# Wide weight tiles and four accumulator banks in the second part of each out projection, and a new slot order for the side work of the last mixer

## What is computed

```python
def second_block(x, norm_mix_w, w_in, ...):
    h = rms_norm_2(x, norm_mix_w)
    proj = h @ w_in                       # 45 column tiles of 128
    z, xbc, dt_raw, q, k, v, f_raw = split(proj)
    y_ssd = ssd_mixer(...)                # 16 heads; (y + d_skip*x) * silu(z), then a norm over two groups
    y_fox = fox_mixer(...)                # 16 heads; q, k normed per head, causal softmax with decays
    x = x + concatenate([y_ssd, y_fox]) @ w_out     # 16 input tiles of 128
    hf = rms_norm_2(x, norm_ffn_w)
    x = x + conv_gated_mlp(hf, w_up, conv_w, conv_b, w_down)

def first_block(x, mem, ...):             # layers 0 (retention) and 1 (differential attention)
    x = x + concatenate([o_main, o_mem]) @ w_out[layer]       # 8 input tiles
    h = rms_norm(x, ffn_norm_w[layer])
    x = x + (silu(h @ w_gate) * (h @ w_up)) @ w_down[layer]
```

## Time and profile before

| | |
|---|---|
| median of 3 runs | 1190.63 us (1189.59 to 1196.57) |
| profiled execution, its own time | 1190.49 us |
| its span (first to last instruction) | 1188.7 us |
| PE busy | 1091.9 us, 92% |
| DVE, ACT, POOL busy | 787.0, 610.2, 170.5 us |
| mean granted TensorE clock | 0.973 |

### The profile page before, as it was taken

The page is one execution under the profiler, slowest core; times in us unless marked ns, Lnnn a source line. Parts: engine busy times, 40 slices in busy tenths (PEclk is TensorE's granted clock), DMA queues, the critical chain, the costliest instruction groups (busy, mean ns, idle before and its releaser), DMA issues.

```text
span 1188.7 us, 23717 instructions
## 1 busy us (share of the span) xinstructions
PE 1091.9 (92%) x8466; PEld 1037.2 (87%) x8466; DVE 787.0 (66%) x1290; ACT 610.2 (51%) x1074; POOL 170.5 (14%) x186
## 2 busy tenths in 40 slices
PE   5999989999998987779999999988788898999999
PEld 5978879999998776679999999987677788999999
DVE  7664676666555785776665658867755648888853
ACT  7643554444544554364444546665544447666542
POOL 4000121111110001031111100000101003444400
PEclk9999989999999998889999999999988999999999
DMA  7522345555664222055555664442222236555563
GB/s 265 176 93 94 92 152 197 185 180 174 190 186 155 77 93 67 27 171 191 179 182 177 181 202 143 163 139 89 89 71 72 78 118 195 179 185 185 168 197 114
DMA packets 52775, 174.45 MB, mean 147 GB/s; under 512 B 5856, under 2 KB 9056, under 8 KB 52576
## 3 DMA queue, kind: packets, MB, share of 16 engines
q1 hardware_dynamic: 52704, 173.49, 45.3%
HBM read 172.42 MB, written 1.05 MB: 146 GB/s over the span
## 4 chain that ended last, share of the span: by engine, by line
PE 50%; DVE 12%; ACT 2%; issue 2%; POOL 0%; ACTq 0%; DVEq 0%
PE bank L561 15%; PE bank L562 15%; PE bank L563 15%; DVE ring_lo L1220 2%; PE bank L614 1%; DVE xw_lo L1226 1%; DVE bank L1367 1%; DVE bank L1365 1%; DVE u L1383 1%; DVE x L1275 1%; DVE negmax L1429 1%; PE bank L700 1%; ACT tmp L1054 1%; PE bank L627 1%; DVE tmp L1426 1%
## 5 line engine op out<-in xcount | busy, mean ns | idle before, releaser
L561 PE MATMUL bank<-xw_hi,ring_hi 128*128 128x256 f32 x1736 | 508.7, 293 | 8.2 <-DVE xw_lo L1226 3.4
L562 PE MATMUL bank<-xw_lo,ring_hi 128*128 128x256 f32 x1736 | 495.4, 285 | 0.0
L563 PE MATMUL bank<-xw_hi,ring_lo 128*128 128x256 f32 x1736 | 495.0, 285 | 0.0
L1220 DVE TENSOR_TENSOR ring_lo<-ring_raw,ring_hi 128x1024 fp32r<-128x1024 f32 (+3 forms) x353 | 399.9, 1136 | 50.1 <-ACT ring_hi L838 43.6
L838 ACT ACTIVATE ring_hi<-ring_raw 128x1024 fp32r<-128x1024 f32 (+3 forms) x353 | 345.0, 979 | 101.1 <-PE bank L563 97.0
L561 PEld LDWEIGHTS bank<-xw_hi,ring_hi 128*128 128x128 f32 x1736 | 337.9, 195 | 17.3 <-issue 10.1
L562 PEld LDWEIGHTS bank<-xw_lo,ring_hi 128*128 128x128 f32 x1736 | 337.7, 195 | 4.1 <-issue 3.9
L563 PEld LDWEIGHTS bank<-xw_hi,ring_lo 128*128 128x128 f32 x1736 | 337.1, 194 | 0.0
L561 PE MATMUL bank<-act_hi,ring_hi 128*128 128x256 f32 x848 | 250.1, 295 | 29.5 <-DVE ring_lo L1220 11.7
L562 PE MATMUL bank<-act_lo,ring_hi 128*128 128x256 f32 x848 | 245.2, 289 | 0.0
L563 PE MATMUL bank<-act_hi,ring_lo 128*128 128x256 f32 x848 | 244.9, 289 | 0.0
(11 more groups left out here) (159 smaller groups left out, 854.6 us busy)
## 6 DMA issues: line engine op xcount, KB each, us to landing
ring_raw<-w_up SPq DMA_DIRECT2D x132, 512.0 KB, 3.2
ring_raw<-w_in SPq DMA_DIRECT2D x85, 512.0 KB, 3.2
ring_raw<-w_down SPq DMA_DIRECT2D x48, 512.0 KB, 3.7
ring_raw<-w_down SPq DMA_DIRECT2D x24, 384.0 KB, 3.9
ring_raw<-w_oa SPq DMA_DIRECT2D x16, 384.0 KB, 3.1
ring_raw<-w_kv SPq DMA_DIRECT2D x8, 512.0 KB, 5.7
ring_raw<-w_oa SPq DMA_DIRECT2D x8, 512.0 KB, 3.5
ring_raw<-w_ob SPq DMA_DIRECT2D x16, 128.0 KB, 2.0
```

The lines of the kernel that those rows point to most:

```text
L561: mm(bank[b][:, 0:T], w_hi, tile(hi, t), start=kk == 0, stop=False)
L562: mm(bank[b][:, 0:T], w_hi, tile(lo, t), start=False, stop=False)
L563: last = mm(bank[b][:, 0:T], w_lo, tile(hi, t), start=False, stop=end)
L1220: V.tensor_tensor(ring_lo[:, a:b], ring_raw[:, a:b], ring_hi[:, a:b].bitcast(f32), SUB).then_inc(lo_done, 1)
```

## The change

It does four things.

1. `PHASES`: ob0 and ob1 have 2 ring tiles of 1024 columns instead of 8 of 256 (four outputs each), ob2 4 of 1024 instead of 8 of 512 (two outputs each). The bytes are the same.
2. ob has its own loops, `project_group` on PE and `group_into_stream` on ACT and DVE. DVE's order is now add of output m, then `xw_lo` of output m-1, with `split_lo` once for each ring tile, behind its last add. ACT's `split_hi` stands behind the square and copy of output `group // 2` of each ring tile.
3. kv, ob, up and down use banks 0 to 3 instead of 0 and 1 (`Phase.bank`), and PE waits for the output four back (`Phase.freed`). in and oa keep two banks.
4. `plans()`, layer 2: `ssd_skip` and `turn` keep their slots but stand first in them; `fox_probs` stands first in its slot or right behind a `norm_out`; `fox_weights`, `fox_values` and the attention's `mix` come one slot later; `group_norm` of the second group moves from slot 37 to 40, with `group_out` and its four `mix` steps (39 to 42).

```diff
-          ("in0", 20, [8], 20), ("oa0", 8, [6], 8), ("ob0", 8, [2], 4), ...
+          ("in0", 20, [8], 20), ("oa0", 8, [6], 8), ("ob0", 2, [8], 2), ...
-          ("in2", 45, [8], 45), ("oa2", 16, [8, 4], 16), ("ob2", 8, [4], 4), ...
+          ("in2", 45, [8], 45), ("oa2", 16, [8, 4], 16), ("ob2", 4, [8], 4), ...
+        self.group = 8 // n if name[:2] == "ob" else 1
+        self.banks = 2 if name[:2] in ("in", "oa") else 4
...
-        at(2, a + 3, "ssd_skip", p)
         at(2, a + 3, "ssd_gate", p)
...
-        at(2, a + 5, "turn", 36 + 2 * j)
-        at(2, a + 6, "turn", 37 + 2 * j)
         for n in range(2):
             p, slot = 2 * j + n, a + 7 + 3 * n
+            plan[2][a + 5 + n].insert(0, ("turn", 36 + p))
             at(2, slot, "fox_scores", p)
-            at(2, slot + 1, "fox_probs", p)
-            at(2, slot + 1, "fox_weights", p)
-            at(2, slot + 2, "fox_values", p)
-            at(2, slot + 3, "mix", 8 + p)
-    for g, slot in ((0, 28), (1, 37)):
+            plan[2][slot + 1].insert(0, ("fox_probs", p))
+            at(2, slot + 2, "fox_weights", p)
+            at(2, slot + 3, "fox_values", p)
+            at(2, slot + 4, "mix", 8 + p)
+    for p in range(8):
+        plan[2][20 + 2 * p].insert(0, ("ssd_skip", p))
+    for g, slot in ((0, 28), (1, 40)):
...
+            def project_group(layer):
+                ph = PH[f"ob{layer}"]
+                ks = DM // P // ph.group
+                for c in range(ph.n):
+                    slot, g = ph.tile(0, c)
+                    pe.wait_ge(lo_done, g + 1)
+                    for j in range(ph.group):
+                        m = ph.group * c + j
+                        n = ph.out0 + m
+                        b = bank[n % 4][:, 0:T]
+                        pe.wait_ge(out_ready, ph.freed_first(n, m))
+                        for k in range(ks):
...
+            def group_into_stream(layer, q):          # ACT
+                ph = PH[f"ob{layer}"]
+                for c in range(ph.n):
+                    for j in range(ph.group):
+                        m = ph.group * c + j
+                        act.wait_ge(out_ready, ph.out0 + m + 1)
+                        stream(q, m, x)
+                        if j == ph.group // 2:
+                            split_hi(ph, 0, c)
...
+            def group_into_stream(layer, q):          # DVE
...
+                        V.tensor_tensor(tile(x, m), tile(x, m), bank[(ph.out0 + m) % 4][:, 0:T], ADD).then_inc(out_ready, 1)
+                        if m:
+                            stream_lo(q, m - 1, x)
+                    split_lo(ph, 0, c)
+                stream_lo(q, KT - 1, x)
```

More of the change, by code:

```diff
@@ L123, in out, with bank, freed, freed_first @@
         return self.out0 + c // self.per + (self.body // self.per) * i
+    def bank(self, i, c):
+        n = self.out(i if type(i) is int else 0, c)
+        return n % self.banks
+    def freed(self, i, c):
+        n, j = self.out(i, c), c // self.per
+        if type(i) is int:
+            j += self.outs // self.turns * i
+        if self.banks == 2 or type(i) is not int and self.outs // self.turns < 4:
+            return n - 1
+        if type(i) is not int or j >= 4 or self.name[:2] in ("up", "do"):
+            return n - 3
+        return self.freed_first(n, j)
+    def freed_first(self, n, j):
+        if j >= 4:
+            return n - 3
+        b = n % 4
+        if b >= 2:
+            return n - j if self.name != "kv" else 0
+        before = self.out0 - 1
+        return (before if before % 2 == b else before - 1) + 1
 def phases():
@@ L545, in project @@
                 n = ph.out(i, c)
-                b = (ph.out0 + c // ph.per) % 2
+                b = ph.bank(i, c)
                 part = c % ph.per
@@ L549, in project @@
                 pe.wait_ge(lo_done, g + 1)
-                if part == 0 and not (first and n < 2):
-                    pe.wait_ge(out_ready, n - 1)
+                if part == 0:
+                    freed = ph.freed(i, c)
+                    if not (type(freed) is int and freed <= 0):
+                        pe.wait_ge(out_ready, freed)
                 last = None
@@ L564, in project @@
                 last.then_inc(tile_done, 1)
+            def project_group(layer):
[10 more added lines that the diff above has]
+                        for k in range(ks):
+                            t = ph.inputs[k]
+                            if m == 0:
+                                pe.wait_ge(mix_lo, number["mix", (layer, t)] + 1)
+                            a = slot * DM + (j * ks + k) * P
+                            w_hi, w_lo = ring_hi[:, a:a + P], ring_lo[:, a:a + P]
+                            mm(b, w_hi, tile(act_hi, t), start=k == 0, stop=False)
+                            mm(b, w_hi, tile(act_lo, t), start=False, stop=False)
+                            last = mm(b, w_lo, tile(act_hi, t), start=False, stop=k == ks - 1)
+                        if j < ph.group - 1:
+                            last.then_inc(ob_done, 1)
+                        else:
+                            last.then_inc(tile_done, 1)
             def mean_square(q):
@@ L1122, in _ @@
                 run(f"oa{layer}", follow(layer, PH[f"in{layer}"].n))
-                run(f"ob{layer}", into_stream(q + 1), unrolled=True)
+                group_into_stream(layer, q + 1)
                 if layer < 2:
@@ L1281, in into_stream @@
                 return after
+            def group_into_stream(layer, q):
+                ph = PH[f"ob{layer}"]
+                for c in range(ph.n):
+                    for j in range(ph.group):
+                        m = ph.group * c + j
+                        if j < ph.group - 1:
+                            dve.wait_ge(ob_done, sum(PH[f"ob{l}"].outs - PH[f"ob{l}"].n for l in range(layer))
+                                        + (ph.group - 1) * c + j + 1)
+                        else:
+                            dve.wait_ge(tile_done, ph.tile(0, c)[1] + 1)
+                        V.tensor_tensor(tile(x, m), tile(x, m), bank[(ph.out0 + m) % 4][:, 0:T], ADD).then_inc(out_ready, 1)
[3 more added lines that the diff above has]
+                stream_lo(q, KT - 1, x)
             def swiglu_evac(layer):
@@ L1599, in _ @@
                     before_split=follow(layer, n_in, MIDDLE))
-                run(f"ob{layer}", add_to_x, into_stream(q + 1), unrolled=True)
+                group_into_stream(layer, q + 1)
                 if layer < 2:
@@ L1648 @@
         w[f"oa{l}"] = column_tiles(rows(w_out, f"oa{l}"))
-        w[f"ob{l}"] = column_tiles(rows(w_out, f"ob{l}"))
+        ob = column_tiles(rows(w_out, f"ob{l}"))
+        ks = ob.shape[1]
+        w[f"ob{l}"] = ob.reshape(ks // P, -1, P, ks).transpose(0, 2, 1, 3).reshape(ks, DM)
         w[f"up{l}"] = interleaved(w_up, FT)
```

9 lines of the change are left out of this document (5 added, 4 removed), and 6 rows, old and new, of the table PHASES.

## The result

The changed kernel takes 1157.09 us (median; 1156.39 to 1157.98), the kernel before 1192.09 beside it. The ratio is 0.970, 95% interval 0.967 to 0.974. The forecast was 1156.

What follows compares the result with a forecast made beforehand. It took PE, 92% busy, to lose time standing behind late results in layer 2 and in ob's serial chain. Terms -31.2, -4.7, -4.3, +1.9, +3.7, -0.5 sum to -35.1 from 1190.5: 1155.4, stated as 1156, range 1147 to 1172 us.

Steps and rivals of the forecast that it cites:

- Layer 2's plan: Slots 27 to 52: 27.8 us of PE waits go, 7 come, half-clock work shrinks; -31.2 us.
- slot 29: Layer 2: division ahead of the state-space weights that `ssd_out` needs makes PE wait 1.9 us.
- The half-clock term: Layer 2, slots 27 to 52: work in six half-clock stretches would take 12.1 us less at full clock.
- ob0 and ob1: Groups of four shorten the chain from first add to last `xw_lo`: -4.7 and -4.3 us.
- the last sum of squares on POOL beside the split: End of each ob: the sum waits for DVE's wide split; estimated 0.7 us each, left out of the sum.
- ob2: Groups of two leave the split behind both outputs with nothing beside it, so the chain lengthens; +1.9 us.
- The clock behind ob: After each ob PE is fed piecemeal by `xw_lo` and its clock falls; 1.0, 1.0 and 1.7, +3.7 us.
- kv's gain: In kv PE no longer waits for its bank, with four banks; -0.5 us.
- signs of being wrong: New PE waits on state-space weights, `norm_out` or `xw_lo` at up's start, or half clock in up's first 5 us.
- The waits did not stay: Rival: layer 2's order changes but producers stay equally late, about -4 us, 1186 us; chance 0.04.
- no up projection started at half rate: Rival: the clock stays down behind ob as up projections begin, 30 us at each of three starts, 1201 us; chance 0.02.
- the first rival: DVE paces layer 2, so 16.7 us of PE waits stay, with ob at -1; 1172 us, chance 0.12.

Runs made afterwards that it cites:

- `e8_fed`: The kernel before, with products of no use ahead of seven steps that wait in layer 2; 1182.71 us, ratio 0.995.
- `e5_ob2_narrow`: The changed kernel with ob2 alone back to eight tiles 512 wide, one output each, its four banks kept; 1154.57 us, ratio 0.970.
- `e6_two_banks`: The changed kernel with four banks in ob alone, two in kv and the up and down projections; 1154.89 us, ratio 0.970.
- `e7_split_order`: The changed kernel with ob's ring splits moved, those of the last group behind everything; 1143.05 us, ratio 0.961.
- `e2_ob_only`: The changed kernel with the old plan of layer 2, so wide ob tiles and four banks alone; 1184.89 us, ratio 0.995.
- the rerun: The changed kernel measured once more, unchanged, beside later runs; 1157.50 us, ratio 0.973.
- `e1_plan_only`: The kernel before with the new plan of layer 2 alone, ob, kv and banks as before; 1160.23 us, ratio 0.975.
- `e3_turn_first`: The kernel before with only the plan's lines on `ssd_skip` and `turn`, which stand first in their slots; 1183.18 us, ratio 0.994.
- `e10_fed`: The kernel of `e9_two_steps` with products of no use ahead of ten waits in layers 0 and 1; 1131.42 us, ratio 0.952.
- `e9_two_steps`: The kernel of `e7_split_order` with two layer 2 steps later: the first `ssd_gate` and the first softmax division; 1139.53 us, ratio 0.959.

## Why the prediction was right

- **Layer 2's plan, -31.2: right, -33.7 in the stage and -31.0 by its own run.** The waits that would remain were named one by one and sized: 0.45 for the copied transposes measured 0.5, 1.1 for the norms 1.05 to 1.09, 1.9 for slot 29 measured 1.3, 0.7 for `group_out` 0.2. In all 5.9 against 7, and no half-clock stretch where one was charged. That waits this short leave the clock up was not a safe step, though: in the trace of before, 3.4 us at half clock follow a wait of 1.78 us (at 62 us). PE's own work was 110.0 us against 110.7. The half-clock term, 12.1 at full size, is shown by `e8_fed`; PE is busy 11.8 us less in the stage.
- **ob0 and ob1, -4.7 and -4.3: right, -4.3 and -3.7.** The chains took 11.3 and 12.2 us against 10.9 and 12.0. What I left out of the sum is the last sum of squares on POOL beside the split. By the rule of the Trainium skill (SBUF — State Buffer, "Who interferes with whom") I had estimated 0.7 each; the last section shows that the rule holds in full, but the last `xw_lo` took 0.95 us for the 0.5 drawn, and the whole chain is only 0.4 and 0.2 us longer. In ob2, 17.6 against 18.25, no sum falls on a split.
- **ob2, +1.9: right, +1.3**, and for the reason given; `e5_ob2_narrow` takes it back in the profile.
- **The clock behind ob, +3.7: right in size (+0.9, +1.1, +1.9), half right in cause.** I put it down to PE being fed piecemeal by `xw_lo`. The one profile of `e6_two_banks` has the same chains and shows 0 behind all three: it is the four banks that let PE begin a tile early and be fed so, standing three times within it. With four banks and `xw_lo` in time (`e7_split_order`) nothing is lost either, so it takes both. Behind ob1 the loss came in one of four such profiles, so that there the size was luck. I had costed the banks at nothing in the up projections; that step was wrong, and it takes back more than kv's gain (1.3, not 0.5). Waits for `xw_lo` and half clock at the start of up, which I had listed as signs of being wrong, did show, at the size that the sum had charged.
- **What the sum did not hold:** +1.65 us in in0 with oa0, +1.5 in in2, and +1.3 before the first product, which kv's gain makes good. I count them to the execution and not to the change, since runs of one and the same program up to there differ as much. With the start of the changed kernel the stretch to the last oa0 add took 156.4 us in `e2_ob_only` and the rerun, as in the profile of after, but 153.0 in `e5_ob2_narrow`; with that of the kernel before it took 154.5 in `e1_plan_only` and 157.9 in `e3_turn_first`. In in2, `e8_fed`, which is the kernel before up to there, took 98.5 us against 96.0. And the first product, at 11.7 us before and 13.0 after, came at 12.6 to 13.1 in the four other runs that start like the kernel before.
- **How near it came.** That the sum is off by only 2 us in 35 is in part luck: layer 2's stage gave 2.5 us more than summed, and the stretches ahead of it, of which the sum had nothing, took more than that back.
- **The rivals.** DVE does not pace the stage: it works 92.7 of 115.9 us, and PE's waits are 5.9, not 16.7. The waits did not stay, and no up projection started at half rate for more than 6.8 us. The sum of the first rival is wrong by its own terms: with 8 for the clock and 2 for the port, ob and kv come to +2.4 and not to -1, so that it gives 1176 and not 1172, and the high end of the range should have been 1176.

## What to carry to other kernels

An engine that runs its instructions in order pays for one late result with all the work queued behind it; ask each result a tile of work later, and price every wait by itself, since here they simply added up. Standing costs twice when the clock falls behind it, 0.43 to 0.47 us for each us at half clock; if a wait can't be moved, products of no use ahead of it gave most of that part back (10.5 us of about 12 in `e8_fed`, 8.1 of 10.8 in `e10_fed`). At the end of a serial chain look for an instruction that nobody needs yet (here the ring split): moving the splits was worth more than widening the tiles.

## What the runs showed of the hardware

**Half clock is not set by the program alone.** The same code with the same wait of 1.78 us, 60 to 72 us from the start, in the profile of after and in that of `e9_two_steps`:

```profile
60.00:72.00 12.00, 10.22 (x47) 7.51 (x46) 6.12 (x12) 3.78 (x9) 0.00 (x0) 0.72 0.25 87
```
```profile
60.00:72.00 12.00, 10.22 (x69) 8.34 (x68) 9.18 (x16) 5.98 (x15) 0.00 (x0) 1.00 0.37 121
```

PE is busy 10.22 us in both, but with 47 products at a clock of 0.72 in the one and 69 at 1.00 in the other. Before the wait both ran at full clock. In `e2_ob_only` and before, the same standing of 27.9 and 27.8 us brought 13.7 and 27.3 us at half clock. Why the clock fell after the wait in one and not in the other was not settled. Much of it does repeat, though: the rerun shows nine of the eleven half-clock stretches of after (without its last 0.7 us) within 0.2 us of the same place, one (at 520.3) not at all, and one (at 786.5) twice as long. That lies between the two outcomes that were put down for it. With the waits filled (`e10_fed`) the clock never fell in the profile, and most of the spread of the times went with it.

**VectorE's split and POOL's sum exclude each other for their whole length.** In ob0 of after:

```profile
165.80 0.74 POOL L1213 TENSOR_TENSOR scratch<-scratch 128x256 f32<-128x256 f32 x1 [0.26 <-ACT scratch L906]
...
167.10 1.22 DVE L1288 TENSOR_TENSOR ring_lo<-ring_raw,ring_hi 128x1024 fp32r<-128x1024 f32 x1 [0.28 <-ACT ring_hi L895]
...
167.45 1.46 POOL L1213 TENSOR_TENSOR scratch<-scratch 128x256 f32<-128x256 f32 x1 [0.92 <-ACT scratch L906]
...
168.25 0.95 DVE L1294 SCALAR_TENSOR_TENSOR xw_lo<-x,par,xw_hi 128x256 fp32r<-128x256 f32 x1
```

And in ob2 of `e7_split_order`:

```profile
948.71 1.23 DVE L1288 TENSOR_TENSOR ring_lo<-ring_raw,ring_hi 128x1024 fp32r<-128x1024 f32 x1 [0.28 <-ACT ring_hi L895]
...
949.06 1.47 POOL L1213 TENSOR_TENSOR scratch<-scratch 128x256 f32<-128x256 f32 x1 [0.92 <-ACT scratch L906]
...
949.86 0.41 DVE L1363 TENSOR_TENSOR x<-x,bank 128x256 f32<-128x256 f32 x1
```

Alone the sum takes 0.74 us. Beside a split it ends 0.66 us after VectorE's next instruction begins (168.91 against 168.25), 0.67 (950.53 against 949.86), and in the earlier trace rows 0.68 (171.22 against 170.54): whenever it started, it works only once the split is over. I had read 0.74 against 1.21 as a part of the rule; it is all of it, since that sum had started later in the split. The `xw_lo` behind the split pays in turn, 0.95 us in ob0 against 0.48 in ob2 of after, where no sum is due.
